# A hybrid decoder step: projection begun tile by tile, forget gate and suffix sums moved into the gates, two loops written out, dense rows turned between products

## The reference

```python
def project(x, pos, lp):
    xn = rmsnorm(x, norm1_g)
    proj = xn @ w_in                    # 1024 x (1536 + 8 + 4608 + 2048)
    q_f, k_f = rmsnorm per head, v_f
    logf = log_sigmoid(parts[3] + b_forget)          # the 8 forget columns
    dil  = (rope(rmsnorm(q)), rope(rmsnorm(k)), v) for each of 3 windows
    return q_f, k_f, v_f, logf, dil, gate_a, gate_b

def finish(x, o_fox, o_dil, gate_a, gate_b, lp):
    mixed = sigmoid(gate_a) * (o_fox @ w_branch_a) + sigmoid(gate_b) * (o_dil @ w_branch_b)
    h = x + mixed @ w_out
    u = relu(rmsnorm(h, norm2_g) @ w_up)
    return h + (u * u) @ w_down
```

## Time and profile before

| | us |
|---|---|
| median of 3 runs | 1981.88 (1981.87 to 1982.9) |
| the profiled execution | 1984.61 |
| its span in the trace | 1982.7 |
| PE busy | 1782.4 (90%) |
| DVE, ACT, POOL busy | 1105.1, 960.5, 825.9 |
| mean granted PE clock | 0.949 of full |

### The profile page before, as it was taken

The page is one execution under the profiler, slowest core; times in us unless marked ns, Lnnn a source line. Parts: engine busy times, 40 slices in busy tenths (PEclk is TensorE's granted clock), DMA queues, the critical chain, the costliest instruction groups (busy, mean ns, idle before and its releaser), DMA issues. The chain is left out here.

```text
span 1982.7 us, 33311 instructions
## 1 busy us (share of the span) xinstructions
PE 1782.4 (90%) x10797; PEld 1565.2 (79%) x10797; DVE 1105.1 (56%) x2531; ACT 960.5 (48%) x1610; POOL 825.9 (42%) x448
## 2 busy tenths in 40 slices
PE   2989999999699999999999976787799699999998
PEld 2877878789688888888888845677698598989897
DVE  4465464721187778788778866767552351515151
ACT  3344443432157777777777755666621331313130
POOL 0143232410017678678677634323333233333331
PEclk8999999999899999999999986888999799999999
DMA  4343526254399999999999846546164366565662
GB/s 171 86 134 119 154 96 198 81 189 133 106 332 317 322 327 322 326 335 318 335 330 313 284 158 200 178 156 221 39 212 170 127 254 251 235 236 235 248 251 111
DMA packets 225243, 426.74 MB, mean 215 GB/s; under 512 B 24473, under 2 KB 85786, under 8 KB 223458
## 3 DMA queue, kind: packets, MB, share of 16 engines
q1 hardware_dynamic: 224258, 423.15, 63.1%
q0 software_dynamic: 864, 2.10, 0.4%
HBM read 392.63 MB, written 119.86 MB: 258 GB/s over the span
## 5 line engine op out<-in xcount | busy, mean ns | idle before, releaser
L902 POOL TENSOR_TENSOR vv_lo<-v_raw,vv_hi 128x1024 fp32r<-128x1024 f32 x178 | 400.5, 2254 | 187.6 <-ACT vv_hi L966 183.0
L1665 POOL TENSOR_TENSOR w_lo<-w_raw,w_hi 128x2048 fp32r<-128x2048 f32 x39 | 180.6, 4631 | 344.6 <-ACT w_hi L1680 344.6
L958 ACT ACTIVATE kt_hi<-ktp 128x1024 fp32r<-128x1024 f32 (+1 forms) x192 | 186.2, 970 | 115.3 <-PE ktp L1118 112.6
L982 DVE TENSOR_TENSOR kt_lo<-ktp,kt_hi 128x1024 fp32r<-128x1024 f32 (+1 forms) x192 | 220.4, 1148 | 9.6 <-ACT kt_hi L958 9.1
L1118 PE MATMUL ktp<-ident,k_raw 128*128 128x128 f32 x1440 | 195.0, 278 | 23.7 <-DMA k_raw<-in_cache_fox_k 23.0
L1118 PEld LDWEIGHTS ktp<-ident,k_raw 128*128 128x128 f32 x1440 | 166.9, 143 | 56.8 <-DMA k_raw<-in_cache_fox_k 28.7
L1134 PE MATMUL s_ps<-kt_hi,q_st 128*128 128x256 f32 (+3 forms) x768 | 205.9, 301 | 0.0
L966 ACT ACTIVATE vv_hi<-v_raw 128x1024 fp32r<-128x1024 f32 (+1 forms) x192 | 191.5, 997 | 10.7 <-PE o_ps L1149 8.0
L565 PE MATMUL acc<-w_hi,xn_hi 128*128 128x512 f32 x480 | 194.1, 404 | 1.7 <-DVE lz_neg L438 1.7
L1134 PE MATMUL s_ps<-kt_lo,q_st 128*128 128x256 f32 (+3 forms) x768 | 190.6, 282 | 0.0
L565 PE MATMUL acc<-w_lo,xn_hi 128*128 128x512 f32 x480 | 189.9, 396 | 0.0
(11 more groups left out here) (224 smaller groups left out, 4219.9 us busy)
## 6 DMA issues: line engine op xcount, KB each, us to landing
k_raw<-in_cache_fox_k SPq DMA_DIRECT2D x256, 256.0 KB, 6.4
v_raw<-in_cache_fox_v SPq DMA_DIRECT2D x256, 256.0 KB, 5.5
out_win_kv_sample<-in_cache_win_kv SPq DMA_DIRECT2D x32, 2040.0 KB, 9.4
w_raw<-in_w_in SPq DMA_DIRECT2D x32, 1024.0 KB, 5.5
k_raw<-in_cache_win_kv SPq DMA_DIRECT2D x40, 512.0 KB, 10.5
v_raw<-in_cache_win_kv SPq DMA_DIRECT2D x40, 512.0 KB, 12.1
w_raw<-in_w_up SPq DMA_DIRECT2D x16, 1024.0 KB, 5.3
w_raw<-in_w_down SPq DMA_DIRECT2D x16, 1024.0 KB, 5.0
```

The source lines that it names most:

```text
L902: gp.tensor_tensor(vv_lo[:, slot, 0:tiles, :], v_raw[:, i % RAW_RING, 0:tiles, :], vv_hi[:, slot, 0:tiles, :].bitcast(F32), ALU.subtract). ...
L958: act.activation(kt_hi[:, slot, :, 0:n], ktp[:, i % 2, :, 0:n], ACT.Copy).then_inc(k_hi, 1)
L982: ve.tensor_tensor(kt_lo[:, slot, :, 0:n], ktp[:, i % 2, :, 0:n], kt_hi[:, slot, :, 0:n].bitcast(F32), ALU.subtract).then_inc(k_lo, 1)
L1665: gp.tensor_tensor(w_lo[:, slot, :], w_raw[:, slot, :], w_hi[:, slot, :].bitcast(F32), ALU.subtract).then_inc(slab_lo_done, 1)
```

## The change

**Start.** x comes in five transfers, one a tile, the first slab between tiles 1 and 2 and the second behind tile 4, ahead of the forget weights. ACT, DVE and PE take the tiles one by one: square, root, scale, turn, high, low. PE starts the first half-chunk's tile 0 with two tiles turned and turns tile t+1 between the products. The first slab's low part is made in two halves, by DVE and by POOL. A square root on `eps_col` loads ACT's table first.

**Moved into the gates.** The gathers (POOL, behind its sets and the last v store), the forget gate (PE, ahead of gate tile 0), its log sigmoid, the page turns (PE at tiles 5 and 7), the suffix sums (PE at tiles 6 and 8), the cumulative sums (tile 9), and SP's stores of them (behind the stores of tiles 8 and 10).

**PE's loop over sets** and, in `finish`, PE's and ACT's loops over groups are Python loops now: the code is written out.

**Dense rows.** `finish` turns tile t-2 behind tile t's product of the last w_out slab, into banks 3 and 5; the high part of slab 8 is made before the squares. The first w_up tile begins with its first half of tokens, then the last two tiles are turned, then the other half.

The core of the diff:

```diff
@@ project_tokens, SP @@
+            load_x(0)
+            sp.dma_start(ident[:], a["c_ident"]).then_inc(ident_in, 16)
+            sp.dma_start(g1_row[:], a["norm1_g"][0].partition_broadcast(P)).then_inc(g1_in, 16)
+            load_x(1)
+            load_slab(0)
+            for t in range(2, TILES):
+                load_x(t)
+            load_slab(1)
...
+            load_slab(N_SLABS + 2)
+            sp.wait_ge(v_stored, 16 * n_v)
+            sp.sem_inc(v_free, 1)
...
+                    if f == 8:
+                        store_suffix(0)
+                        store_forget()
+                    if f == 10:
+                        store_suffix(1)
@@ POOL @@
+            gp.wait_ge(slab_hi_done, 1)
+            rest = slice(SLAB // 2, SLAB)
+            gp.tensor_tensor(w_lo[:, 0, rest], w_raw[:, 0, rest], w_hi[:, 0, rest].bitcast(F32), ALU.subtract).then_inc(slab0_lo_rest, 1)
...
+            gp.wait_ge(idx_in, 16 * LF_GROUPS)
+            gp.wait_ge(v_free, SETS + 1)
@@ ACT @@
+            mean_square(0)
+            mean_square(1)
+            x_turned_hi(0)
+            split_hi(1, 0)
+            for t in range(2, TILES):
+                mean_square(t)
+                x_turned_hi(t - 1)
+            split_hi(1, 1)
+            x_turned_hi(TILES - 1)
...
+                if f in (5, 7):
+                    i = (f - 5) // 2
+                    act.wait_ge(yt_stored, 16 + 16 * 10 * SETS)
+                    act.wait_ge(lf_turned, i + 1)
+                    act.activation(lf_t[:, i], tp[:].rearrange("p a (h n) -> p (a h) n", n=P), ACT.Copy).then_inc(lf_kept, 1)
...
                 last.then_inc(gate_done, 1)
+                forget_job(f)
@@ PE @@
+                if f == 5:
+                    pe.wait_ge(lz_step, 1)
+                    turn_pages(0)
+                if f == 6:
...
+                    pe.wait_ge(lf_kept, 1)
+                    sum_suffix(0)
+                if f == 7:
+                    pe.wait_ge(sfx_kept, 1)
+                    turn_pages(1)
+                if f == 8:
+                    pe.wait_ge(lf_kept, 2)
+                    sum_suffix(1)
...
+                    if first:
+                        if 1 <= t < TILES - 1:
+                            turn_x(t + 1)
+                        pe.wait_ge(x_lo_done, 2 * t + 2)
...
-            with pe.Fori(0, SETS) as s:
+            for s in range(SETS):
@@ finish, ACT @@
             slab_part(7, 4, 1)
+            act.wait_ge(half_used, 2)
+            slab_part(8, 5, 0)
@@ finish, PE @@
+            def turn_behind(t):
+                if t >= TURN_LATE:
+                    turn_rows(t - TURN_LATE)
...
+                    if g == 0 and f == 0:
+                        pe.wait_ge(hn_lo, 2 * 3)
+                        up(0, (0,))
+                        for t in range(TILES - TURN_LATE, TILES):
+                            turn_rows(t)
+                        up(1, (0,))
+                        pe.wait_ge(hn_lo, 2 * TILES)
+                    first_of_all = g == 0 and f < 2
+                    up(f, (1,) if first_of_all else range(HALVES)).then_inc(up_done, 1)
```

More of the change, by code:

```diff
@@ L509, in _, with turn_x @@
             pe.sem_inc(gate_done, 2)
-            pe.wait_ge(consts_in, N_CONSTS)
-            for i in range(LF_GROUPS):
+            def turn_x(t):
+                pe.wait_ge(x_scaled, t + 1)
+                for u in (2 * t, 2 * t + 1):
+                    if u >= 2:
+                        pe.wait_ge(x_lo_done, u - 1)
+                    for k in range(4):
+                        last = pe.transpose(tp[:, u % 2, k * P:k * P + P], x_in[:, t, (4 * (u % 2) + k) * P:(4 * (u % 2) + k + 1) * P], ident[:])
+                    last.then_inc(x_turned, 1)
@@ L512, in _, with sum_suffix, turn_pages @@
+            def sum_suffix(i):
+                for h in range(HEADS):
+                    last = pe.matmul(tp[:, h // 4, (h % 4) * P:(h % 4 + 1) * P], lf_t[:, i, h, :], tri[:], start=True, stop=True)
+                last.then_inc(sfx_summed, 1)
+            def turn_pages(i):
                 pe.wait_ge(lf_gathered, 16 * (i + 1))
                 for h in range(HEADS):
-                    last = pe.transpose(acc[:, 2 * i + h // 4, (h % 4) * P:(h % 4 + 1) * P], lf_rows[:, i, h, :], ident[:])
+                    last = pe.transpose(tp[:, h // 4, (h % 4) * P:(h % 4 + 1) * P], lf_rows[:, i, h, :], ident[:])
@@ L515, in _ @@
                 last.then_inc(lf_turned, 1)
[L516 to L520, removed]
-                for k in range(4):
-                    last = pe.transpose(tp[:, u % 2, k * P:k * P + P], x_in[:, t, (4 * half + k) * P:(4 * half + k + 1) * P], ident[:])
-                last.then_inc(x_turned, 1)
-            pe.wait_ge(wf_lo_done, 1)
@@ L533, in _ @@
-            last.then_inc(z_summed, 1)
-            def sum_suffix(i):
-                for h in range(HEADS):
-                    last = pe.matmul(acc[:, 2 - 2 * i + h // 4, (h % 4) * P:(h % 4 + 1) * P], lf_t[:, i, h, :], tri[:], start=True, stop=True)
-                last.then_inc(sfx_summed, 1)
-            pe.wait_ge(sfx_consts, 32)
-            pe.wait_ge(page_summed, LF_GROUPS)
-            pe.matmul(acc[:, 4, 0:LF_GROUPS * HEADS], later[:], page_sum[:].rearrange("p g h -> p (g h)"), start=True, stop=True).then_inc(later_summed, 1)
@@ L1833, in _, with turn_rows, natural @@
                 last.then_inc(branch_done, 1)
-            def natural(n, c, half, before):
+            def turn_rows(t):
+                pe.wait_ge(hn_done, t + 1)
+                for u in (2 * t, 2 * t + 1):
+                    if u >= 2:
+                        pe.wait_ge(hn_lo, u - 1)
+                    for k in range(4):
+                        last = pe.transpose(acc[:, 3 + 2 * (u % 2), k * P:k * P + P], hn[:, t % 2, (4 * (u % 2) + k) * P:(4 * (u % 2) + k + 1) * P], ident[:])
+                    last.then_inc(hn_turned, 1)
+            def natural(n, c, half, before, behind=None):
                 pe.wait_ge(slab_lo_done, n + 1)
```

352 lines of the change are left out of this document (192 added, 160 removed).

## The result

The changed kernel took 1932.1 us, the median of four executions (1930.8 to 1934.0), against 1981.9 for the kernel before: a ratio of 0.9748, with a 95% interval of 0.9736 to 0.9761. Later executions, on two chips, gave 1937.8 and 1936.2, ratios 0.9780 (0.9761 to 0.9798) and 0.9774 (0.9761 to 0.9787). Over all of them the changed kernel's mean is 1935.6 (14 executions) and that of before 1981.9 (46), which is 46.3 us. The forecast was 35.8 us, 1946.1, and its range ended at 1938. So the direction was right, and about 10 us of the gain were not in the sum.

A forecast was written before the change was run, and what follows sets the result against it. The prediction took TensorE (PE), busy for 90% of the span, as the bound. -44.0 + 16.7 - 8.5 + 0 = -35.8 us from 1984.61 gave 1948.8, less 2.7 to the median 1946.1; 8-in-10 range 1938 to 1955.

The forecast's parts named there:

- Start, forecast -44.0: Start up to set 0's gap: first projection product at 17.9, gap ending at 65.1 instead of 109.14, 44.0 us earlier.
- 28.9: Set 0: us from the end of the first half-chunk (36.2) to the gap's end, taken from set 1 of before.
- The halves of slab 0: Start: DVE's and POOL's halves run one after the other, 1.22 + 2.25 us; side by side PE would begin at 16.7.
- Gates, forecast +16.7: Gates: 13.2 us of PE work moved in at full clock, plus 3.5 of new waits.
- The two waits: Gates, tiles 6 and 8: PE waits 1.75 us each for ACT's page copy behind the sigmoid, 3.5 in all.
- rival 1: Gates: the clock falls in the two new waits, +5.0 us, giving 1951.1; chance 0.12.
- POOL's gathers: Gates: two gathers, 16 us, hidden in the 38 us until tile 5; otherwise PE waits for the remainder.
- Dense part, forecast -8.5: Last stage: third w_up tile (f=2) starts at 1574.5 instead of 1583.0, 8.5 us; 6 or 11 depending on half clock.
- The first w_up product: Last stage: first w_up matmul expected 12 us earlier against the end of the branch products than before.
- The sets, forecast 0: Sets beyond the start: no term in the sum, so their length was held as before.
- the loops: PE's two loops and ACT's written out: 0 us, no stall at set or group turns or from code arriving.
- both ends better: Start and dense part both do better, 2.5 us at the start and 11 in the dense part: 1941; chance 0.10.

The follow-up runs named there:

- a0: The changed kernel itself, unaltered, run again on another chip than its first four executions: 1937.8 us.
- a1: The changed kernel itself, unaltered, run once more, beside a second run of e2: 1936.2 us.
- e2: The changed kernel with one Ln ahead of ScalarE's loop over the sets, putting its table loads back: 1939.2 us, then 1936.8 beside a1.
- e5: The changed kernel with the low part of weight slab 0 made whole by VectorE, none by GpSimd: 1934.7 us beside a0's 1937.8.
- e3: The kernel before with only the loops written out (TensorE's over sets and feed-forward groups, ScalarE's over groups): 1979.1 us against 1982.1, ratio 0.9982.
- e1: The kernel before with one extra square root ahead of ScalarE's loop over the sets, keeping its function table: 1975.1 us against 1982.1, ratio 0.9968.
- e7: The changed kernel with VectorE's split for a set's second half-chunks ahead of the last rotation product: 1919.4 us beside a0's 1937.8.

## Why the prediction was too small

**Start, forecast -44.0.** Right in mechanism and in size. The first product starts at 17.47 (17.9). ACT's next slab split, which starts where the first half-chunk ends, is at 35.50 (36.2; 36.30 and 35.99 in a0 and a1). From there the prediction added 28.9 to the end of set 0's gap, taken from set 1 of before, and that span had a table load at its head. In the changed kernel it is 27.4 in all three traces; with the load put back (e2) it is 28.7 in both. So the gap ends at 62.90 (65.1), 63.3 by the mean of three traces, 45.9 earlier than the mean of the old starts, 109.2. Of these 45.9 the table load is 1.3 and the written-out loop 0.2; what is left, 44.4, is close to the 44.0 that was forecast. The halves of slab 0 ran one after the other, as the rows of before had suggested, and e5 shows the price.

**Gates, forecast +16.7.** Measured +16.2, from K1 to the end of the gates. The two waits are 1.59 and 1.72 (1.75) with the clock at 1.00, so rival 1 is out; POOL's gathers were hidden.

**Dense part, forecast -8.5.** 8.4 between the means of the traces. The first w_up product came 10.5 us earlier and not 12. Tile f=2 of w_up, the third, on which the 8.5 was reckoned, starts 136.4 to 136.5 us behind the first branch product in the traces with the new stage, against 143.7 in before and 145.2 in e3: 7.2 to 8.8 earlier.

**The sets, forecast 0: the step that failed.** The sum held the sets at their old length, beyond the start, and carried the 28.9 over with the words "Set 0 now has the same queue". They became 6.1 us shorter in the traces (285.7 against 291.8, K0 to K1), and 1.5 more lie ahead of K0. Of these 7.6, four table loads are 5.1, eight waits of TensorE that end sooner in the written-out code are 1.4, and the rest, about 1, is half clock, which differs between executions. I had asked of the loops only whether a turn or the code's arrival stalls PE, and found rightly that neither does. I had not asked what else a loop does. Two things: a wait in it ended 0.18 later, and, the larger, ScalarE's loop, which the change leaves a loop, carried two table loads in each pass, one of them on the path, because of what stood ahead of it. The row was in my hands: "From ACT's table load at 168.30" is in the working, as a mark to measure from. A load of 1.28 us on the path in each of four passes, in a loop whose functions never change, should have made me ask who puts another table there: the Exp and Ln that this very change moves away. I counted table loads that the move adds in the gates and not those that it takes from the loop.

**The sum at means.** -45.9 (start) - 6.1 (sets) + 16.2 (gates) - 8.4 (last stage) - 1.7 (attention, not more than its spread) = -45.9, and -46.3 was measured over all executions. Of the 10.1 that this is beyond the forecast of -35.8, the failed step is 7.6 and the attention's spread 1.7. The first four executions of the changed kernel were in the mean 3.4 us below its mean of fourteen. Whether that was their chip or their luck stays open; without it the time would still have been below the range, by 2.4 us. The range was too narrow since none of its cases let a stage that was put at 0 gain anything: its best case, both ends better, was 1941.

## What to carry to other kernels

When a change moves an activation function across a loop, compare the function tables at the loop's entry and at its end: if they differ, the body can pay a load in each pass, as it did here, and one dummy activation ahead of the loop takes it away (e1). Where PE is at its limit, follow each short, regular gap back through the engine that ends it. Here the order of two operations on VectorE (e7) was worth 18 us, more than the dense part and the loops of this change together. And before a stage that no edit touches is given a cause, look at its length in several executions.

## What was not expected of the hardware

- The clock behind a gap is not set by the gap's length alone: behind gaps of 2.12 and 2.14 in one execution the next 10 us ran at 0.84 and 1.00, and in a0 all four ran at 0.83. Equal code lost 4.9 and 8.8 us to it. Counted over the first stage of all traces, by the mean clock of the 8 us behind the gap: after 17 gaps of 1.6 to 1.75 it stayed at 1.00 each time; after 23 of 2.10 to 2.14 it fell 19 times; after 11 of 3.4 it fell 4 times, after 6 of 3.59 5 times. So the gaps of 3.4 cost less often than those of 2.1, and what decides stays open.
- A GpSimd product that takes 1.29 alone took 3.41 beside a VectorE split of 2.29, as if the loser of the two waited for the other's whole instruction (its 1.29 behind a 2.29 would be 3.58); one engine alone made the slab of 2048 columns in 2.29, the two together in 3.44.
- A function table load on ScalarE's path cost its 1.28 in the gap and nothing behind it; the second one in a pass was nearly free in the shadow of a wait.
- The same attention code, with the same transfers, took 900.9 to 908.0 us.
